# Two decoder blocks on one core: transposes in other batches, other banks in the second block's output projection, and one engine fewer in two residual additions

## The reference, cut to what matters

```python
h = rms_norm(x, g_mix_pre); proj = h @ w_in           # queries, keys, values, recurrence, two gates
merged = sigmoid(gate_a) * (y_attn @ w_attn_branch) + sigmoid(gate_b) * (y_hgrn @ w_hgrn_branch)
x = x + rms_norm(merged @ w_out, g_mix_post)                        # end "ffn": next comes the FFN
h = rms_norm(x, g_ffn_pre); gate, up = split(h @ w_gate_up)
x = x + rms_norm((silu(gate) * up) @ w_down, g_ffn_post)            # end "ple"
e = (p @ w_ple_proj) * sigmoid(rms_norm(x, g_ple_pre) @ w_ple_gate)
x = x + rms_norm(e, g_ple_post)                                     # end "mix2": next, block two
...
x = x + concat(o_a, o_b) @ w_o                                      # o0, o1: eight heads each
x = x + conv_ffn(rmsnorm(x, norm2_g), w_up, conv_w, conv_b, w_down) # gate2, value2, down2
return rmsnorm(x, final_g)
```

## Time and profile before

| what | value |
|---|---|
| median of 3 runs | 2692.86 us (2690.43 to 2692.99) |
| the profiled execution | 2694.51 us, its span 2692.4 us |
| TensorE busy | 2658.9 us, 99% of the span |
| VectorE, ScalarE busy | 1885.0 us (70%), 1525.1 us (57%) |
| GpSimd busy | 81.6 us (3%), in three stretches |
| granted TensorE clock, mean | 0.996 of full speed |
| DMA | 493.02 MB, 183 GB/s, queues busy 58% |

### The profile page before, as it was taken

How to read it: one execution, slowest core, us unless ns; L and a number is a source line. 1 busy time by engine, 2 the same in 40 slices (tenths; PEclk the granted TensorE clock), 3 DMA queues, 4 the chain that set the end, 5 groups by cost and what they waited for, 6 DMA issues and landing times.

```text
span 2692.4 us, 38802 instructions
## 1 busy us (share of the span) xinstructions
PE 2658.9 (99%) x13882; PEld 2253.2 (84%) x13882; DVE 1885.0 (70%) x3527; ACT 1525.1 (57%) x2956; POOL 81.6 (3%) x96
## 2 busy tenths in 40 slices
PE   9999999999999999999999999999999999999998
PEld 7888888878888888888887888888788888888887
DVE  6776567565777567657757678666688758866885
ACT  6674535445655455545547665554566546655664
POOL 0000000000300000000003200000000000000000
PEclk9999999999999999999999999999999999999999
DMA  7454545656556666566555555544556566556665
GB/s 270 144 163 150 172 149 184 219 170 223 186 188 188 204 205 188 192 190 187 188 189 180 169 168 173 163 144 162 172 175 193 187 196 188 188 188 190 188 192 157
DMA packets 136816, 493.02 MB, mean 183 GB/s; under 512 B 15704, under 2 KB 16216, under 8 KB 135856
## 3 DMA queue, kind: packets, MB, share of 16 engines
q1 hardware_dynamic: 134064, 479.98, 56.5%
q0 software_dynamic: 2272, 10.31, 1.3%
q10 hardware_dynamic: 288, 0.26, 0.0%
HBM read 488.37 MB, written 4.21 MB: 183 GB/s over the span
## 4 chain that ended last, share of the span: by engine, by line
PE 93%; DVE 3%; ACT 1%; DMA 1%; POOL 1%; issue 1%; DVEq 0%; SPq 0%; ACTq 0%; POOLq 0%
PE bank L592 92%; DMA raw<-in_ws_mix 1%; DVE lo L1576 1%; POOL arena L2393 0%; ACT hi L1046 0%; DVE arena L1576 0%; PE bank L631 0%; POOL X L2397 0%; DVE arena L1579 0%; ACT sq_t L1153 0%; DVE arena L2211 0%; PE bank L705 0%; DVE X L1579 0%; DVE X L1576 0%; PE bank L670 0%
## 5 line engine op out<-in xcount | busy, mean ns | idle before, releaser
L1576 DVE TENSOR_TENSOR lo<-raw,hi 128x512 fp32r<-128x512 f32 x1804 | 1240.1, 694 | 745.5 <-ACT hi L1046 651.0
L1046 ACT CAST hi<-raw 128x512 fp32r<-128x512 f32 x1804 | 1108.4, 620 | 936.3 <-PE bank L592 914.1
L592 PE MATMUL bank<-XS,hi 128*128 128x512 f32 x3760 | 1038.0, 397 | 3.4 <-DVE u_t L1576 1.3
L592 PEld LDWEIGHTS bank<-XS,hi 128*128 128x128 f32 x3760 | 644.0, 189 | 96.8 <-issue 5.9
L592 PEld LDWEIGHTS bank<-XS,lo 128*128 128x128 f32 x3760 | 577.5, 189 | 79.9
L592 PE MATMUL bank<-XS,lo 128*128 128x256 f32 x3760 | 599.4, 281 | 0.0
L592 PE MATMUL bank<-hi,HS 128*128 128x512 f32 x1952 | 546.8, 391 | 2.6 <-DVE X L1576 2.6
L592 PEld LDWEIGHTS bank<-hi,HS 128*128 128x128 f32 x1952 | 364.9, 188 | 78.1 <-issue 3.8
L592 PE MATMUL bank<-hi,XS 128*128 128x512 f32 x1472 | 412.9, 395 | 0.7 <-DVE XS L1579 0.3
L592 PE MATMUL bank<-lo,HS 128*128 128x512 f32 x976 | 322.4, 390 | 3.0 <-DVE lo L1576 3.0
L592 PEld LDWEIGHTS bank<-hi,XS 128*128 128x128 f32 x1472 | 273.2, 189 | 60.5 <-ACT hi L1046 3.7
(11 more groups left out here) (193 smaller groups left out, 1014.8 us busy)
## 6 DMA issues: line engine op xcount, KB each, us to landing
raw<-in_ws_ffn SPq DMA_DIRECT2D x528, 512.0 KB, 3.6
raw<-in_ws_mix SPq DMA_DIRECT2D x338, 512.0 KB, 3.6
raw<-in_ws_ple SPq DMA_DIRECT2D x35, 512.0 KB, 3.7
arena<-in_gains POOLq DMA_DIRECT2D x4, 1024.0 KB, 7.9
arena<-in_xt SPq DMA_DIRECT2D x8, 256.0 KB, 6.2
X<-in_xt POOLq DMA_DIRECT2D x1, 2048.0 KB, 10.1
t5rows<-t5row POOLq DMA_DIRECT2D x8, 256.0 KB, 5.1
out<-arena SPq DMA_DIRECT2D x8, 256.0 KB, 3.0
```

The lines of the kernel that those rows point to most:

```text
L592: return eng.matmul(o, l, r, start=start, stop=stop, skip_group_check=True)
L1046: eng.copy(hi[:, b % SPL, :], raw[:, u % RAW, part * BW:(part + 1) * BW]).then_inc(halved.next(b), 1)
L1576: return eng.tensor_tensor(o, a, b, op)
```

## The change

Four edits, all in what is placed where.

1. **Ticks of transposes.** Keys: transposed at TURN + 7 (before + 3), copied at + 8 (before + 4). Second queries, first half of the heads: transposed at + 3 (before + 5), copied at + 4 (before + 6); their second half stays at + 7 and + 8. First queries stay at + 3. Merged branches: transposed four ticks behind the quarter (before three), taken out at five (before four).
2. **Banks of `o1`.** They follow the same rule as `o0`: (1, 7), (2, 0), (1, 7), (2, 0).
3. **The ring behind the four.** The four groups of the second FFN bring the ring back to bank 0, so `gate2` 2 goes to bank 0 (before 1), `value2` 2 to bank 1 (before 2), and so on through the FFN.
4. **The ends.** At "ffn" and "mix2" VectorE makes all eight steps; GpSimd keeps steps 3 to 7 of "ple" alone. A new rule (`made_at`) places them.

```diff
-OWN_PARTS = 3
+OWN_PARTS = {"ffn": 8, "ple": 3, "mix2": 8}
...
-         "o0": None, "o1": [(0, 1), (2, 7), (0, 1), (2, 7)],
+         "o0": None, "o1": None,
...
-                    elif g.kind == "o0":
+                    elif g.kind in ("o0", "o1"):
                         own = self.by["bv", 1].banks[0]
                         g.banks = (own, 7) if g.q % 2 == 0 else ((own + 1) % 3, (own + 2) % 3)
...
                     elif four and g.kind in ("gate2", "value2"):
                         g.bank = (0, 1, 6, 2)[k]
+                        ring += -ring % 3
...
             s = step_of(c)
-            return added if s < OWN_PARTS else filled, (name, s)
+            return added if s < OWN_PARTS[name] else filled, (name, s)
+
+        def made_at(name, s):
+
+            _, g, e = ENDS[name]
+            return g.last + s - 3 if s - 3 <= BEFORE[name] else e + STEPS[s][0] // P - 4
...
             def turn(g):
-                yield TURN[g.i] + (5 if g.i == 2 else 3) - (g.last + 1)
+                yield TURN[g.i] + (7 if g.i == 0 else 3) - (g.last + 1)
...
             def merge(g):
-                yield 3
+                yield 4
...
                 for k, o in enumerate(a_turned[g.i]):
-                    yield at + (6 + 2 * k if g.i == 2 else 4 + k) - g.last
+                    yield at + (8 if g.i == 0 else 4) + (4 * k if g.i == 2 else k) - g.last
...
             def merged(g):
-                yield 4
+                yield 5
...
                 chunks_at = [entered_at(name, c) for c in range(NC)]
-                for tick in sorted(set(chunks_at)):
+                parts_at = {s: made_at(name, s) for s in range(3, OWN_PARTS[name])}
+                for tick in sorted(set(parts_at.values()) | set(chunks_at)):
                     yield tick - (g.last - 1)
...
+                    for s, at in parts_at.items():
+                        if at == tick:
+                            for m in range(2):
+                                make(s, m)
...
-                for s in range(OWN_PARTS, len(STEPS)):
+                for s in range(OWN_PARTS[name], len(STEPS)):
...
-            on.wait_ge(in_x2, 0)
-            make_rest("ffn")
...
-            for name in ("ple", "mix2"):
-                make_rest(name)
+            make_rest("ple")
```

## The result

The changed kernel takes 2681.44 us (median of 5 runs, 2679.91 to 2681.80) against 2692.99 us for the kernel before (5 runs of the same measurement, 2690.43 to 2694.55). That is 11.55 us less, a ratio of 0.9956 with a 95% interval of 0.9942 to 0.9971. The forecast was 2681.0 in a range of 2676 to 2687. The profiled execution of the changed kernel took 2679.91 us, that of the kernel before, whose rows stand above, 2694.51: the two traces are 14.6 us apart, 3.1 more than the medians, and what follows keeps the two differences apart.

What follows compares the result with a forecast made beforehand. The prediction took TensorE, through its idle time and clock, to bound the kernel. Its terms, 2.6 + 3.8 + 3.9 + 0.2 + 0.8 + 0.3 + 0.2 = 11.8 us, taken off a median of 2692.86, gave 2681.0, range 2676 to 2687.

Steps and rivals of the forecast that it cites:

- What bounds the kernel: TensorE, busy 2658.9 of 2692.4 us, so only its 33.5 us of idle time and its clock can give anything.
- Keys: At the keys, waits of 2.10 us and a slow stretch (1.7) go, a new 1.2 comes at the first queries: gain 2.6.
- Second queries: At the second queries, the 2.08 us wait for ScalarE's copy and the slow stretch behind it go: gain 3.8.
- Merged branches: At the four merged branches, all four waits for the sums go with transposes one batch later: gain 3.9 us.
- Banks of `o1`: Wait before `o1` moves to the second FFN's first matmul, 2.6 us with a slow stretch behind it: gain 0.2.
- The ring: At `gate2` 2, the 1.31 us wait ends 0.8 sooner because bank 0 is read earlier than bank 1: gain 0.8.
- First FFN's entry: At the first FFN, GpSimd's 1.34 us wait goes, a new 1.1 comes at the split of chunk 3: net gain 0.3.
- Second block's entry: At the second block, the same steps move to VectorE, mostly an earlier first batch: gain 0.2 us.
- A: At the second FFN's start, the moved wait does not come, `o1`'s term is 4.5: 2676.7 us, chance 0.12.
- C: At both ends, all ten added VectorE instructions delay the splits: 5.4 us slower, 2698.3, chance 0.03.
- B: The clock falls elsewhere or less often: 2679.3 us with one slow stretch fewer, 2682.7 with one more, chance 0.18.
- D: At keys and branches, waits return one or two instructions later: gains of 1 to 5, 2688 to 2692 us, chance 0.12.

Runs made afterwards that it cites:

- the four single edits: The kernel before with one part changed each: merged branches 2687.72 us, second queries 2689.16, keys 2690.74, banks of `o1` 2692.95.
- the first combined kernel: The changed kernel with bank 6 in `o1`, keys two batches later instead of four, and the first FFN's residual steps 3 to 5 made late: 2674.75 us.

## Why the prediction was right, point by point

- **What bounds the kernel.** Right. Every gain came at the predicted places, from TensorE's idle time, from its clock, or from what a wait costs beside its idle time, which I had left out. VectorE's total changed by 1 us and mattered nowhere else.
- **Keys.** Forecast 2.6, lined up 2.9 in the changed kernel and alone, 2.8 by the runs. The new wait was 1.01 where I had 1.2, released by ScalarE's third copy as said. The 1.7 in it was a slow stretch that comes in some executions only (next section).
- **Second queries.** Forecast 3.8, lined up 3.8 in the changed kernel and alone, 4.4 by the runs. Right in both parts, the wait and the slow stretch.
- **Merged branches.** Forecast 3.9, lined up 4.8. The mechanism was right, and this was the largest mis-sized term: I took the idle time (0.99) for the cost (1.21), four times.
- **Banks of `o1`.** Forecast 0.2 with the wait moved (2.6 before the FFN's first matmul, the slow stretch behind it). Measured 2.57, 3.3 us at 0.50, and 0.4 in all. Alone the medians give 0.6, which can't be told from nothing. This is the point where the edit, looked at by itself, should have gained 4.5, and looking at what used bank 0 next saved the forecast.
- **The ring.** Forecast 0.8 and a wait of 0.5, lined up 0.8 and 0.52. It was not tried alone.
- **First FFN's entry.** Forecast net 0.3, lined up 1.2 (1.3 against the kernel with only this undone). With the branches it is the other large mis-sized term, in three parts. The new wait cost the 1.1 that I had (0.87 of it shown as idle). The entry's own was 0.37 shorter, which I had named but not put into the sum. And GpSimd's steps cost 1.9 where I had 1.34: 1.6 at the wait, the same kind of error as at the branches, and 0.3 at the chunks just ahead of it.
- **Second block's entry.** Forecast 0.2, lined up 0.2. I had the clock as a chance, but not what a missing slow stretch would uncover: GpSimd's wait of 1.64. The change takes away this wait, which the profile of before did not list: the first combined kernel has no slow stretch there either, and no such wait. One reading was wrong. I wrote that the waits of 1.3 us and less have no slow stretch behind them, but just ahead of the fourth one (1535.7) the trace of before has three gaps that my list left out:

```profile
1533.28 0.44 PE L631 MATMUL bank<-cst,X 128*128 128x128 f32 x2 [1.32 <-DVE X L1579]
1534.07 0.66 PE L631 MATMUL bank<-cst,X 128*128 128x128 f32 x4 [0.35 <-DVE X L1579]
1535.36 1.72 PE L592 MATMUL bank<-XS,hi 128*128 128x512 f32 x4 [0.63 <-DVE XS L1579]
```

- **Rivals.** A is out by the changed trace and by `o1` alone. C did not happen where the change puts the steps, but its mechanism is real one entry further on, for 3.0 us in all. B is partly true: which executions show a slow stretch at the keys varies (next section). D is out.
- **The total.** The terms sum to 11.8 and the lined-up traces to 14.6, of which 0.4 is the first batches. So I was short by 2.4 at the places themselves, 0.9 of it at the branches and 0.9 at the first FFN's entry. The medians of the four single edits give 5.9 + 4.4 + 2.8 + 0.6 = 13.7 without the ends and the ring. That 11.8 met the medians' 11.55 to 0.3 us is partly luck: the profiled execution of before was 1.5 above the median here, that of the changed kernel 1.5 below. One known part is that before's execution had a slow stretch at the keys, which two of the four traces with the keys unmoved don't have. The rest of the 3.1 us, which executions have which stretches, was not seen, since only one execution of each kernel has a trace.

## What to carry to other kernels

When an edit gives a tile or bank a new order, follow the old one's last user to the next writer: a bank wait tends to move, not go, and the trace of before has the sum's end to price it. Size a wait of a pipelined engine from the start of the instruction ahead of it to the start of the one behind, in a place with and one without the wait, not by its idle time, and ask of every slow or late stretch whose waits it hides. Work given to an engine with room belongs just ahead of the one who needs it, not as soon as it can be made: here the same steps gained 1.2 us, 2.3 us with a later place in VectorE's queue, and lost 3.0 at an entry where all of them came first.

## What the runs showed of the hardware

**The granted clock follows standing still, but not like a rule.** Over the fourteen traces of this study (the kernel before, the changed one, twelve experiments), a slow stretch at 1.2 GHz came with each of the 15 waits of 2.08 us or longer. It began between 0.4 us before the wait's end and 1.4 us after. It came with the keys' 1.5 in 2 of 4 traces, the gaps at the second block's entry (1.3, 0.35, mostly 0.43 to 0.63) in 11 of 13, the 1.22 at the third entry in 2 of 13, and none of the 23 waits of 1.0 us at the branches or the first queries. The length alone does not order them: none of the 18 waits of 1.3 to 1.64 us at the first FFN's entry, at `gate2` 2 and for GpSimd had one. Once it came with no idle time that the profile shows, behind short matmuls (1815 in the combined kernel). A stretch always lasted 3.3 to 3.4 us and cost at most 1.7. The Trainium skill ("TensorE: Matmul & The Clock Gate", "What's actually happening") says that the watching is not tied to the kernel's start. Equal gaps with and without a slow stretch agree with that and don't prove it.

**The first batches vary by 3 us.** The same matmul, behind 24 of the large products, started at 23.17 in the trace of the second queries alone and at 26.11 in that of bank 6 in `o1`. ScalarE's casts wait for the first weight transfers there, 6.8 and 8.1 us in total, but the trace of before has 5.4 us and its matmul at 24.19, so the sum of these waits alone does not set it. 33 runs of the kernel before lie between 2691.18 and 2696.16, a scatter of some 2.5 us either way, so edits of a microsecond were told by lining traces up and not by times.
